# First expert group of a PEER feed-forward block: the order in which two gathered rows are issued

## The reference

```
q = (xb @ w_query) -> 8 heads x 2 halves        # block of 128 tokens
sc = q . sub_keys                               # 128 keys per half
top 16 of each half, top 16 of their 256 sums -> idx (16 experts a head)
g = softmax(top_s)
a = gelu(einsum('thkd,td->thk', expert_u[idx], xb))
out = einsum('thk,thkd->td', g * a, expert_v[idx])
```

## Time and profile before

| | before |
|---|---|
| median of 3 runs | 1851.31 us (1850.42 to 1851.76) |
| profiled execution | 1852.81 us |
| its span | 1851.0 us |
| PE, DVE, ACT, POOL busy | 85%, 59%, 22%, 47% |
| bytes moved | 648.38 MB, mean 350 GB/s |
| mean granted clock of PE | 0.981 |

### The profile page before, as it was taken

How to read it: one execution, slowest core, us unless ns; L and a number is a source line. 1 busy time by engine, 2 the same in 40 slices (tenths; PEclk the granted TensorE clock), 3 DMA queues, 4 the chain that set the end, 5 groups by cost and what they waited for, 6 DMA issues and landing times.

```text
span 1851.0 us, 16313 instructions
## 1 busy us (share of the span) xinstructions
PE 1566.7 (85%) x5476; PEld 924.6 (50%) x5478; DVE 1097.6 (59%) x1535; ACT 406.4 (22%) x586; POOL 861.3 (47%) x1091
## 2 busy tenths in 40 slices
PE   8999999999978989987777767777777777877897
PEld 8998888789634444443222223222222233333486
DVE  6667645557675555655565555656556665554755
ACT  4435445332101010110111101011110101111254
POOL 1000000001767856767666756666666756576400
PEclk9999999999999999999999989999999999999999
DMA  7445545868999999999999999999999999999952
GB/s 256 160 144 175 175 133 170 283 216 283 418 422 419 421 419 422 418 419 419 421 422 422 421 422 422 421 422 422 422 422 422 422 422 421 422 409 422 387 196 77
DMA packets 130630, 648.38 MB, mean 350 GB/s; under 512 B 14156, under 2 KB 14264, under 8 KB 64264
## 3 DMA queue, kind: packets, MB, share of 16 engines
q0 software_dynamic: 74640, 542.41, 70.7%
q1 hardware_dynamic: 55728, 105.09, 16.8%
q10 hardware_dynamic: 200, 0.06, 0.0%
HBM read 645.42 MB, written 2.10 MB: 350 GB/s over the span
## 4 chain that ended last, share of the span: by engine, by line
POOL 31%; issue 24%; PE 24%; DMA 16%; DVE 2%; ACT 1%; POOLq 0%; DVEq 0%; ACTq 0%; SPq 0%
DMA v_ring<-in_peer_v_dram,idxv 12%; PE acc L1614 12%; POOL u_ring L485 9%; POOL v_ring L492 9%; POOL tick L491 8%; PE acc L1645 4%; DMA u_ring<-in_peer_u_dram,idxu 4%; POOL tick L484 3%; PE mix L1614 2%; PE acc L1933 2%; POOL v_ring L504 1%; DVE u_ring L1368 1%; POOL u_ring L498 1%; PE mix L1933 1%; PE mix L1688 1%
## 5 line engine op out<-in xcount | busy, mean ns | idle before, releaser
L1368 DVE CUSTOM_DVE_ANT_0 u_ring<-u_ring,xn 128x2048 f32<-128x2048 f32 x252 | 577.5, 2292 | 453.6 <-DMA u_ring<-in_peer_u_dram,idxu 452.4
L1933 PE MATMUL mix<-v_ring,diag 128*128 128x512 f32 x1024 | 487.3, 622 | 122.7 <-DMA v_ring<-in_peer_v_dram,idxv 105.8
L1933 PE MATMUL acc<-v_ring,diag 128*128 128x512 f32 x960 | 442.1, 605 | 138.8 <-DMA v_ring<-in_peer_v_dram,idxv 135.4
L1933 PEld LDWEIGHTS mix<-v_ring,diag 128*128 128x128 f32 x1024 | 194.2, 197 | 384.1 <-issue 257.7
L1933 PEld LDWEIGHTS acc<-v_ring,diag 128*128 128x128 f32 x960 | 174.8, 191 | 403.9 <-issue 225.9
L491 POOL TENSOR_TENSOR tick<-tick 128x1 f32<-128x1 f32 x224 | 186.6, 833 | 281.3 <-PE acc L1933 152.1
L485 POOL DMA_INDIRECT u_ring<-in_peer_u_dram,idxu x224 | 238.2, 1064 | 35.4 <-issue 31.5
L820 ACT ACTIVATE diag<-ident,wgt 128x128 f32<-128x128 f32 x224 | 86.0, 398 | 764.3 <-PE mix L1933 383.5
L492 POOL DMA_INDIRECT v_ring<-in_peer_v_dram,idxv x224 | 223.6, 998 | 35.4 <-issue 9.1
L975 DVE TENSOR_TENSOR w_lo<-raw,w_hi 128x2048 fp32r<-128x2048 f32 x63 | 144.4, 2292 | 140.3 <-ACT w_hi L604 139.1
L604 ACT ACTIVATE w_hi<-raw 128x2048 fp32r<-128x2048 f32 x64 | 122.4, 1914 | 204.9 <-PE acc L1614 147.6
(11 more groups left out here) (339 smaller groups left out, 1548.6 us busy)
## 6 DMA issues: line engine op xcount, KB each, us to landing
raw<-in_w_in_dram SPq DMA_DIRECT2D x48, 1024.0 KB, 5.1
raw<-in_w_out_dram SPq DMA_DIRECT2D x16, 1024.0 KB, 5.3
raw<-in_w_ple_gate_dram SPq DMA_DIRECT2D x16, 1024.0 KB, 6.0
raw<-in_peer_query_dram SPq DMA_DIRECT2D x5, 1024.0 KB, 5.4
qw_u<-in_peer_query_dram SPq DMA_DIRECT2D x4, 1024.0 KB, 15.1
qw_v<-in_peer_query_dram SPq DMA_DIRECT2D x4, 1024.0 KB, 9.1
u_ring<-in_peer_u_dram,idxu POOLq DMA_INDIRECT x256, 16.0
v_ring<-in_peer_v_dram,idxv POOLq DMA_INDIRECT x248, 14.9
```

What stands on the lines that cost most here:

```text
L1368: V.tensor_tensor_reduce(out=u_ring[:, k % DEEP, :], in0=u_ring[:, k % DEEP, :], in1=xn2[:, b, :], scale=1.0, scalar=0.0, op0=ALU.mult, op ...
L1933: ins = T.matmul(pairs[j // 2][:, (j % 2) * CW:(j % 2 + 1) * CW], diag[:, k % DEEP, :], v_ring[:, k % DEEP, j * CW:(j + 1) * CW], start=Fa ...
```

## The change

U row 4 is issued in front of U row 3, and V row 0 in front of U row 7. The copy of the indices for V moves behind the fifth issue of the sequence: it stood between rows 3 and 4, and it stands between rows 4 and 3. The waits go with their rows. The order in which the vector engine takes its products (0, 1, 2, 3, 4, ...) is the same, as are all other engines' programs.

```diff
-                    for k in range(AHEAD):
+                    for k in (0, 1, 2, 4, 3, 5, 6):
                         if k < DEEP - 1:
                             pool.wait_ge(u_slot_read, k + 1)
                         if k == DEEP - 1:
                             pool.wait_ge(q_ready, 2)
                         row_u(0, 0, k)
-                        if k == DEEP - 1:
+                        if k == DEEP:
                             nc.gpsimd.tensor_copy(idxv[:, 1, :], idxu[:, 0, :]).then_inc(idx_moved, 1)
                     pool.wait_ge(idx_moved, 1)
                     for k in range(DEEP):
...
                         row_v(0, 1, k)
+                        if k == 0:
+                            row_u(0, 0, AHEAD - 1)
                         row_u(0, 0, AHEAD + 2 * k)
                         row_u(0, 0, AHEAD + 2 * k + 1)
```

## The result

| | before | after |
|---|---|---|
| median | 1851.57 us (18 runs, 1849.99 to 1857.10) | 1854.78 us (18 runs, 1852.22 to 1856.49) |
| profiled execution | 1852.81 us | 1856.49 us |
| its span | 1851.0 us | 1854.7 us |

The changed kernel is slower: ratio 1.0016, 95% interval 1.0010 to 1.0023, that is +3.0 us (1.9 to 4.3). The prediction said 1851.9 us, with 1853.8 as its upper end.

A forecast was written before the change was run, and what follows sets the result against it. Gather transfers at 421 GB/s bound the kernel. The 1.0 us gain becomes +0.6 us through row 8's late landing, with V's swap at 0: 1852.81 + 0.6 = 1853.4, median 1.5 lower, 1851.9 us; range 1849.5 to 1853.8.

The forecast's parts named there:

- The frame: Expert part: gathers run at 421 GB/s; only idle DMA time ahead or a new hole in the stretch moves the end.
- Rows in the queue land 1.0 us sooner, position by position: Start of the gathers: issuing row 4 early fills the hole at 458-460 us, a gain of 1.0 us.
- Row 3's landing: U row 3, now fifth in line, lands at 465.4 us, making product 3 late by 2.85 us.
- Its lower bound of 1.0 us: Least lateness of product 3, from row 3 landing no sooner than 463.5 us, 4.86 us after its issue ends.
- It lands 4.45 us later, at 479.45: U row 8: issue falls under product 5, ends at 475.0; landing at 479.45 against 478.83 before gives +0.6 us.
- rival A: Row 8's issue slips ahead of product 5, or product 3 is only 1 us late; gain kept, 1850.3 us; chance 0.33.
- all is shifted by one constant below 1 us: Sign that the forecast is right: from 480 us on, everything moves by the same small amount.
- Rival B: The hole repeats as issues behind row 8 fall under products: +4.2 us, 1855.5 us; chance 0.06.
- V's swap, put at 0: V row 0 goes ahead of U row 7, whose wait for product 3 hides the cost: 0, from -0.3 to +0.5 us.

The follow-up runs named there:

- the held run: Kernel before, with U row 5 and all behind it not issued until U row 4 has landed; 1854.72 us against 1851.74, ratio 1.0017.
- late by 1.2: Kernel before with one filler reduction of 128x1024 on the vector engine ahead of product 3; 1852.33 us against 1851.36, ratio 1.0003.
- copy behind row 3: Changed kernel with the copy of V's indices put after U row 3 instead of ahead of it; 1853.91 us against 1851.73, ratio 1.0013.
- late by 3.2: Kernel before with two filler reductions on the vector engine ahead of product 3, gathers in old order; 1855.09 us against 1851.73, ratio 1.0017.
- rows 4 and 3 alone: Kernel before with only U rows 4 and 3 swapped, V row 0 still behind U row 7; 1854.47 us against 1851.73, ratio 1.0017.
- row 5 ahead too: Changed kernel with U row 5 also issued in front of U row 3; 1856.75 us against 1851.74, ratio 1.0025.

## Why the prediction was wrong, step by step

**The frame held.** The steady stretch moves 421 GB/s whatever is done ahead of it, and the loss is the transfer time lost in front: 3.85 us by the 54 us window, 3.7 by the span, 3.2 by the median.

**The issue times up to row 6 held to 0.1 us.** Row 4 at 454.76 forecast, 454.78 found; the copy to end by 456.8, found 456.77; row 3 from 456.9 to 458.66, found 456.94 to 458.71. Row 6, said to stay, stayed (461.36 against 461.29). V row 0 went at 464.60 against a forecast 464.0.

**"Rows in the queue land 1.0 us sooner, position by position" failed.** The fifth row in line landed just before 466.23, where row 4 had landed at 466.37: 0.1 us, not 1.0; over all profiles it landed 19.1 to 20.6 us after row 0's issue in the new order, 19.1 to 19.9 in the old one. The fourth in line gained nothing either. By 464 us both kernels had moved the same within 24 KB in the 16 windows from 448 us (5170 and 5146 KB). Row 4's head start filled half of 458-460, and thin windows at 460-463 took it back. I had treated the queue as one server that delivers at 421 GB/s as soon as it has a row; it doesn't do so for the last part of a row (131 and 25 GB/s in 464-466 us of the held run, with row 4 not yet landed). (Row 4 "in hand from about 456.7" has no row behind it: 455.73 + 4.45 - 2.49 is 457.7. That is still ahead of row 2's landing, so the argument doesn't hang on it.)

**Row 3's landing was thereby 465.4 in place of 466.2**, and the lateness of product 3 2.85 in place of 3.67 us, 3.1 to 4.6 in the other profiles with rows 4 and 3 swapped. Its lower bound of 1.0 us, built on the 4.86 us of a row with "nothing ahead of it", was no possibility: even with nothing behind row 3, product 3 was 3.3 us late. Nor was the queue empty ahead of those rows: row 1 landed only at 454.84, after row 2's issue had ended.

**"It lands 4.45 us later, at 479.45" was right in its sum by luck.** Row 8's issue didn't fall under product 5 but slipped in 0.03 us ahead of it (472.60, product at 472.63), took 0.94 us and ended at 473.54, 1.5 us earlier than the forecast: rival A's race came out as A had it. The row then landed just before product 8's start at 479.96, some 6.4 us after the issue's end and not 4.45. The two errors nearly cancel, and product 8 is 1.2 us late where +0.6 was said, with +1.0 as a bound. A's gain didn't follow, for it stood on the same 4.45 us. On the race itself, the Trainium skill (SBUF — State Buffer, "Who interferes with whom") has it that whichever is issued first gets the ports and the other waits. This trace agrees down to 0.03 us for the issue, which was not held up. It doesn't for the product, which ran 2.29 us as always and started 2.59 us after product 4 (2.61 before).

**The step that failed in the sum is the end of it: one hole at row 8, "grown a little", and behind it "all is shifted by one constant below 1 us".** The sum priced everything behind row 8 at nothing (at most 0.5 us, for row 10). The trace shows the lateness growing there: product 8 by 1.2 us, product 9 by 1.6, product 10 by 2.7, product 12 by 3.2, and 3.7 us at the end of the span. What I left out is that each later release hangs on product 3, so its lateness reaches every row behind it, and it turns into lost transfer nearly one for one. The doses: 1.2, 3.1, 3.2, 3.7, 4.5 and 6.3 us of lateness lost 1.4, 3.3, 3.2, 3.85, 4.1 and 6.4 us of transfer (late by 1.2, copy behind row 3, late by 3.2, after, rows 4 and 3 alone, row 5 ahead too). Only where the products were changed was it less: 4.6 us of lateness lost 2.7 with products in halves, and some 3.8 us lost 1.8 to 1.9 with product 4 taken first.

**Rival B, at 0.06, was near in price and in part in mechanism.** The issues of U 9, V 1, U 10 and U 11 fell under products and took 3.00, 1.91, 2.35 and 2.77 us; V 2 and U 12 didn't (0.94 us each), and the loss is +3.0 us against B's +4.2. I put it low on the argument that a late row leaves GpSimd free to issue fast. It does so once, at row 8. But B had the held-up issues make the loss, and the runs show the lateness of product 3 as the cause and those issues as a part of unsettled size.

**V's swap, put at 0, was 0 as far as a time can tell**: 0.04 us between medians, with an interval of -1.1 to 2.2 us.

## What to carry to other kernels

When a stretch is limited by transfers and its ring of buffers is refilled by what the consumer frees, look at the consumer's order, not at the queue's idle time. Here, putting an early-ready item in front of the one that the consumer wanted next cost that item's lateness, and while the queue was still shallow nearly all of it turned into lost transfer, far behind the place where it arose: follow a late release through every later one and not to the first hole alone. A landing priced from a nearly empty queue must not be used for an item issued close behind another: take the nearest row with the same neighbour ahead, subtract nothing from it, and allow for its scatter, 1 to 2 us here.

## What the runs showed of the hardware

A gather of 1.049 MB whose issue ended with at most 1.9 us of the row ahead still to come landed 4.45 to 4.86 us after its issue ended (rows 0 to 3 of before); one issued closer behind another (3.0 us or more still to come, where it could be read) landed 6.5 to 8.4 us after, and 7.2 and 7.3 us with nothing behind it. An issue on GpSimd that began 0.03 us ahead of a vector product took 0.94 us, and the product was not delayed; one that began 0.10 us behind (475.20, product at 475.10) took 3.00.
